# A decoder block's mixer: channel sums in pairs, two subtractions on GpSimd, the first convolution tap on ScalarE, and another order of VectorE's work

## Time and profile before

| | |
|---|---|
| median of 3 runs | 1147.88 us (1146.88 to 1148.16) |
| the profiled execution's own time | 1145.58 us |
| its span, first to last instruction | 1143.8 us |
| mean granted TensorE clock | 0.992 of full speed |
| TensorE matmul busy | 1102.6 us (96%) |
| VectorE busy | 334.3 us (29%) |
| ScalarE busy | 231.9 us (20%) |
| GpSimd busy | 23.0 us (2%) |
| HBM | 391 GB/s over the span |

### The profile page before, as it was taken

The page is one execution under the profiler, slowest core; times in us unless marked ns, Lnnn a source line. Parts: engine busy times, 40 slices in busy tenths (PEclk is TensorE's granted clock), DMA queues, the critical chain, the costliest instruction groups (busy, mean ns, idle before and its releaser), DMA issues.

```text
span 1143.8 us, 14032 instructions
## 1 busy us (share of the span) xinstructions
PE 1102.6 (96%) x5779; PEld 529.0 (46%) x5779; DVE 334.3 (29%) x639; ACT 231.9 (20%) x332; POOL 23.0 (2%) x34
## 2 busy tenths in 40 slices
PE   8999999999999999999999999999999999999997
PEld 8999998433333333333333333333333333333336
DVE  7899996311111111111111111111111111111127
ACT  7555454211110010110000010110100000000026
POOL 1300000000000000000000000000000000000011
PEclk9999999999999999999999999999999999999999
DMA  9984589899999999999999999999999999999991
GB/s 305 333 310 150 183 320 379 357 416 410 424 431 427 433 426 435 425 437 424 438 424 438 424 438 424 438 424 429 433 435 426 435 426 434 423 425 429 427 398 58
DMA packets 40959, 447.62 MB, mean 391 GB/s; under 512 B 3427, under 2 KB 3675, under 8 KB 21755
## 3 DMA queue, kind: packets, MB, share of 16 engines
q1 hardware_dynamic: 39924, 444.43, 93.5%
q0 software_dynamic: 672, 1.99, 0.7%
q10 hardware_dynamic: 327, 0.69, 0.2%
HBM read 446.05 MB, written 1.05 MB: 391 GB/s over the span
## 4 chain that ended last, share of the span: by engine, by line
PE 68%; DMA 28%; ACT 2%; DVE 1%; SPq 1%; issue 1%; DVEq 0%; ACTq 0%
PE ps L2038 23%; PE ps L2078 16%; DMA down_ring<-in_expert_w_down_dram 13%; DMA up_ring<-in_expert_w_up_dram 13%; PE ps L1765 6%; PE ps L2089 4%; PE ps L1775 3%; PE ps L1952 3%; DMA up_ring<-in_ple_gate_w_dram 2%; PE ps L1829 2%; PE ps L2194 2%; PE ps L1855 1%; ACT hT L985 1%; PE ps L1834 1%; PE ps L2066 1%; PE ps L2049 1%
## 5 line engine op out<-in xcount | busy, mean ns | idle before, releaser
L2038 PE MATMUL ps<-up_ring,hT 128*64 128x512 f32 x2032 | 447.2, 596 | 11.0 <-DMA up_ring<-in_expert_w_up_dram 10.6
L2038 PEld LDWEIGHTS ps<-up_ring,hT 128*64 128x64 f32 x2032 | 148.2, 138 | 301.5 <-issue 281.1
L2078 PE MATMUL ps<-down_ring,hT 128*64 128x512 f32 x992 | 229.8, 605 | 16.6 <-DMA down_ring<-in_expert_w_down_dram 10.1
L1515 DVE TENSOR_SCALAR extra<-ps 128x512 f32<-128x512 f32 x32 | 22.1, 692 | 698.0 <-PE ps L2049 698.0
L2078 PEld LDWEIGHTS ps<-down_ring,hT 128*64 128x64 f32 x992 | 68.1, 138 | 153.4 <-issue 139.6
L981 ACT ACTIVATE work<-ps 128x512 f32<-128x512 f32 x31 | 18.5, 596 | 424.1 <-PE ps L2049 424.1
L2089 PE MATMUL ps<-hT,extra 64*128 64x512 f32 x256 | 72.0, 640 | 0.8 <-DVE hT L1546 0.8
L1765 PE MATMUL ps<-h_hi,w_hi 128*128 128x256 f32 x288 | 70.2, 284 | 0.0
L1765 PE MATMUL ps<-h_lo,w_hi 128*128 128x256 f32 x288 | 69.9, 283 | 0.0
L791 ACT ACTIVATE w_hi<-up_ring 128x2048 fp32r<-128x2048 f32 x28 | 53.4, 1914 | 59.7 <-PE ps L1775 29.4
L481 DVE TENSOR_TENSOR w_lo<-up_ring,w_hi 128x2048 fp32r<-128x2048 f32 x28 | 64.3, 2301 | 3.8 <-ACT w_hi L791 3.6
(11 more groups left out here) (315 smaller groups left out, 804.6 us busy)
## 6 DMA issues: line engine op xcount, KB each, us to landing
up_ring<-in_expert_w_up_dram SPq DMA_DIRECT2D x47, 4096.0 KB, 27.0
down_ring<-in_expert_w_down_dram SPq DMA_DIRECT2D x63, 2048.0 KB, 18.3
up_ring<-in_expert_w_up_dram SPq DMA_DIRECT2D x31, 2048.0 KB, 15.1
up_ring<-in_w_in_dram SPq DMA_DIRECT2D x21, 1024.0 KB, 6.7
up_ring<-in_branch_w_dram SPq DMA_DIRECT2D x6, 1024.0 KB, 5.0
up_ring<-in_w_out_dram SPq DMA_DIRECT2D x4, 1024.0 KB, 6.8
up_ring<-in_expert_w_up_dram SPq DMA_DIRECT2D x4, 1024.0 KB, 24.2
up_ring<-in_ple_gate_w_dram SPq DMA_DIRECT2D x4, 1024.0 KB, 25.2
```

The lines of the kernel that those rows point to most:

```text
L1515: nc.vector.tensor_scalar(lin, ps[:, LIN, :], 1.0 + LIMIT, 1.0 - LIMIT, ALU.min, ALU.max).then_inc(lin_ready, 1)
L2038: ins = nc.tensor.matmul(ps[64 * g:64 * g + 64, GLU + side, :], xe[:, j, k % 4, k // 4, :], gated_columns(w, side, g), start=(k == 0), sto ...
L2078: last = nc.tensor.matmul(ps[64 * g:64 * g + 64, Y, :], actT[:, r, c, :], down_units[:, c, D * r + 512 * g:D * r + 512 * (g + 1)], start=( ...
```

## The change

- `mean_of_channels` takes two matmuls in place of four: GpSimd first adds tiles 0 and 1 to tiles 2 and 3 (`channel_pair_sums`, an addition of 128 x 512), once for `convT` and once for `squares`.
- The first mean is made behind branch unit 22 in place of ahead of it, the second behind unit 23 in place of behind 22. VectorE's `centred` stands behind its split of unit 24.
- Both `bias_rest` go from VectorE to GpSimd, the first ahead of the `rw` product; ScalarE's `round_biases(1)` goes from chunk a to behind chunk pool and its split of unit 8.
- The first tap of the convolution (scale and bias) is made by ScalarE; VectorE waits for it.
- ScalarE copies `pT` and `sguT` out of PSUM in place of VectorE.
- `v_norm` takes four `scalar_tensor_tensor` of 128 x 512 in place of six operations.
- `sgu_product` stands behind VectorE's split of unit 17, `yc_lo` behind that of unit 20, and `yc_hi` on ScalarE behind chunk 8.
- The semaphore `fold_ready` is replaced by a third count of `fills_ready`.

```diff
-BIAS_UNIT, SGU_UNIT = 16, 9
+SGU_PRODUCT_UNIT, YC_UNIT = 17, 20
...
+        channel_pairs = work[:, 2048:2560].rearrange("p (g t) -> p g t", g=2)
...
@@ gpsimd
+            def bias_rest(step):
+                rows = slice(0 if step == 0 else 2 * N_EXP, BIAS_PARTS * N_EXP)
+                pool.wait_ge(b_rounded, step + 1)
+                nc.gpsimd.tensor_tensor(b_rest[rows, :], b_rest[rows, :], b_parts[rows, :], ALU.subtract
+                                        ).then_inc(b_rest_ready, 1)
+            bias_rest(0)
             pool.wait_ge(mats_loaded, 64)
...
                                     ALU.mult).then_inc(rw_ready, 1)
+            pool.wait_ge(rw_ready, 1)
+            bias_rest(1)
+            def channel_pair_sums(src):
+                return nc.gpsimd.tensor_tensor(channel_pairs[:, :, :], src[:, 0:2, :], src[:, 2:4, :], ALU.add)
+            pool.wait_ge(b_rest_ready, 2)
+            pool.wait_ge(ycT_ready, 1)
+            pool.wait_ge(conv_step, CT * CONV_K)
+            channel_pair_sums(convT).then_inc(channel_pairs_ready, 1)
+            pool.wait_ge(mean_done, 1)
+            pool.wait_ge(sq_ready, 1)
+            channel_pair_sums(squares).then_inc(channel_pairs_ready, 1)
...
@@ scalar
                 if name == "a":
-                    round_biases(1)
+                    act.wait_ge(a_read, 1)
+                    act.wait_ge(taps_ready, 1)
+                    for c in range(CT):
+                        b = ROW["conv_b"] + c
+                        nc.scalar.activation(convT[:, c, :], y_pad[:, c, 0:T], ACT.Identity, bias=prm[:, b:b + 1],
+                                             scale=conv_taps[:, 0, c:c + 1]).then_inc(conv_step, 1)
                     continue
...
+                if n == 2:
+                    round_biases(1)
+                if n == 4:
+                    act.wait_ge(early_T_done, 1)
+                    nc.scalar.activation(pT[:, :, :].rearrange("p a t -> p (a t)"), ps[:, 4, :], ACT.Copy)
+                    nc.scalar.activation(sguT[:, :, :].rearrange("p h t -> p (h t)"), ps[:, 5, :], ACT.Copy
+                                         ).then_inc(sguT_ready, 1)
+                if n == 8:
+                    act.wait_ge(ycT_ready, 1)
+                    nc.scalar.activation(yc_hi[:, :, :], uT[:, :, :], ACT.Copy).then_inc(yc_hi_ready, 1)
...
             nc.scalar.activation(squares[:, :, :], convT[:, :, :], ACT.Square).then_inc(sq_ready, 1)
-            act.wait_ge(ycT_ready, 1)
-            nc.scalar.activation(yc_hi[:, :, :], uT[:, :, :], ACT.Copy).then_inc(yc_hi_ready, 1)
             split(BRANCH_UNIT0 + 3)
...
@@ vector
-                if u == 3:
-                    bias_rest(0)
...
-            for c in range(CT):
-                b = ROW["conv_b"] + c
-                nc.vector.tensor_scalar(convT[:, c, :], y_pad[:, c, 0:T], conv_taps[:, 0, c:c + 1],
-                                        prm[:, b:b + 1], ALU.mult, ALU.add).then_inc(conv_step, 1)
+            dve.wait_ge(conv_step, CT)
...
-                    own(nc.vector.tensor_scalar(v_sb[:, a, :], v_sb[:, a, :], vmv[:, 2 * a:2 * a + 1],
-                                                vrstd[:, a:a + 1], ALU.subtract, ALU.mult))
-                    own(nc.vector.tensor_tensor(v_sb[:, a, :], v_sb[:, a, :], v_gain, ALU.mult))
-                    last = nc.vector.tensor_tensor(v_sb[:, a, :], v_sb[:, a, :], v_shift, ALU.add)
+                    own(nc.vector.scalar_tensor_tensor(out=v_sb[:, a, :], in0=v_sb[:, a, :],
+                                                       scalar=vmv[:, 2 * a:2 * a + 1], in1=v_gain,
+                                                       op0=ALU.subtract, op1=ALU.mult))
+                    last = nc.vector.scalar_tensor_tensor(out=v_sb[:, a, :], in0=v_sb[:, a, :],
+                                                          scalar=vrstd[:, a:a + 1], in1=v_shift,
+                                                          op0=ALU.mult, op1=ALU.add)
...
-                if u == BIAS_UNIT:
-                    bias_rest(1)
...
-                if u == SGU_UNIT:
-                    dve.wait_ge(early_T_done, 1)
-                    nc.vector.tensor_copy(pT[:, :, :].rearrange("p a t -> p (a t)"), ps[:, 4, :])
-                    nc.vector.tensor_copy(sguT[:, :, :].rearrange("p h t -> p (h t)"), ps[:, 5, :]).then_inc(sguT_ready, 1)
+                if u == SGU_PRODUCT_UNIT:
+                    sgu_product()
+                if u == YC_UNIT:
+                    dve.wait_ge(yc_hi_ready, 1)
+                    nc.vector.tensor_tensor(yc_lo[:, :, :], uT[:, :, :], yc_hi[:, :, :].bitcast(F32),
+                                            ALU.subtract).then_inc(yc_lo_ready, 1)
...
             split(BRANCH_UNIT0)
-            dve.wait_ge(mean_done, 1)
-            nc.vector.tensor_tensor(convT[:, :, :], convT[:, :, :],
-                                    ps[:, 4:5, 0:T].to_broadcast([P, CT, T]), ALU.subtract).then_inc(centred, 1)
-            sgu_product()
             split(BRANCH_UNIT0 + 1)
-            dve.wait_ge(yc_hi_ready, 1)
-            nc.vector.tensor_tensor(yc_lo[:, :, :], uT[:, :, :], yc_hi[:, :, :].bitcast(F32),
-                                    ALU.subtract).then_inc(yc_lo_ready, 1)
...
             split(BRANCH_UNIT0 + 2)
+            dve.wait_ge(mean_done, 1)
+            nc.vector.tensor_tensor(convT[:, :, :], convT[:, :, :],
+                                    ps[:, 4:5, 0:T].to_broadcast([P, CT, T]), ALU.subtract).then_inc(centred, 1)
             dve.wait_ge(chunk_read, N_CHUNKS - 1)
             gate_branch(0)
...
@@ tensor
+            def mean_of_channels(bank):
+                for c in range(2):
+                    last = nc.tensor.matmul(ps[:, bank, 0:T], mean_mat[:, :], channel_pairs[:, c, :], start=(c == 0),
+                                            stop=(c == 1))
                 return last
...
-                    if u == BRANCH_UNIT0 - 1:
-                        pe.wait_ge(conv_step, 4 * CONV_K)
-                        pe.wait_ge(yaT_ready, 1)
-                        mean_of_channels(4, convT).then_inc(mean_done, 1)
...
                 if i == 0:
-                    pe.wait_ge(sq_ready, 1)
-                    mean_of_channels(5, squares).then_inc(var_done, 1)
+                    pe.wait_ge(yaT_ready, 1)
+                    pe.wait_ge(channel_pairs_ready, 1)
+                    mean_of_channels(4).then_inc(mean_done, 1)
+                if i == 1:
+                    pe.wait_ge(channel_pairs_ready, 2)
+                    mean_of_channels(5).then_inc(var_done, 1)
```

More of the change, by code:

```diff
@@ L382, in build @@
         mean_done = sem("mean_done")
+        channel_pairs_ready = sem("channel_pairs_ready")
         centred = sem("centred")
@@ L395, in build @@
         first_copied = sem("first_copied")
-        fold_ready = sem("fold_ready")
         logits_done = sem("logits_done")
@@ L1125, in _ @@
             nc.vector.tensor_reduce(fold[:, :], ident[:, :].rearrange("p (c e) -> p e c", c=4), axis=AX,
-                                    op=ALU.add).then_inc(fold_ready, 1)
+                                    op=ALU.add).then_inc(fills_ready, 1)
             for a in range(TT):
@@ L1926, in _ @@
             w_out_tile(m + 1, 1, [1]).then_inc(w_used, 2)
-            pe.wait_ge(fold_ready, 1)
+            pe.wait_ge(fills_ready, 3)
             pe.wait_ge(x_ready, 2)
```

## The result

The changed kernel takes 1154.59 us (median of 6 runs, 1152.19 to 1156.03) against 1146.85 us for the kernel before on the same chips: ratio 1.0063, 95% interval 1.0053 to 1.0072, so 7.2 us slower (6.1 to 8.3); the two medians differ by 7.7. The forecast was 4.2 us slower, 1152.1 us, its range 1148.5 to 1156.0 us.

The account below looks back on a forecast made before the run. TensorE was taken to bound the mixer, VectorE 3 to 5 us ahead, then the DMA stream. VectorE's lateness of 7.9 less 0.8 us, through layer norm's chain, gave +4.2 us: 1152.1 us, range 1148.5 to 1156.

Parts of the forecast that it names:

- Step 3: `bias_rest(0)` on GpSimd, 44.1 to 48.5 us, makes VectorE's taps stand: +4.4 us, and the `rw` product +0.5.
- Step 4: `bias_rest(1)` on GpSimd, 56.7 to 61.1 us, holds VectorE +4.4 us; TensorE stands 3.2 us for unit 8.
- the cushion: VectorE's 2.61 us of idle time ahead of 54.33 us in the kernel before, forecast to be used up.
- Step 5: VectorE's operations spared and put in front, together -0.8 us; the split of unit 22 starts at 147.1 us.
- Rival A: GpSimd is in nobody's way and VectorE keeps its lead: -1.6 us, 1146.3 us; chance 0.14.
- rival B: Only TENSOR_TENSOR stands, taps run beside GpSimd: +1.9 us, 1149.8 us; chance 0.15.
- rival C: Worse: a bf16 input costs GpSimd more, or TensorE's clock falls: up to +8 us, 1156 us; chance 0.13.
- Step 7: TensorE stands from 170.7 to 172.1 us ahead of unit 26, before at 167.90: +4.2 us, nothing changed behind it.
- Step 6: Layer norm's chain: first pair sum 1.15 us, done at 150.4; `centred` done at 156.0, `yb_lo` at 172.1 us.
- The sign that I had set for being wrong: GpSimd waits through a whole row of VectorE instructions, making `b_rest_ready` and ScalarE's split of unit 9 late; no size.
- Step 2: First tap on ScalarE: four activations of 1.58 us, done at 38.75 us, VectorE 1.6 us later.
- Step 1: Means: eight float32 matmuls become four, -1.73 us on TensorE.

Follow-up runs that it names:

- e1: The changed kernel with both `bias_rest` back on VectorE: 1149.04 us, ratio 1.0017 to the kernel before.
- e7: As e6, with `yb_lo` ahead of `gate_branch(2)` and of the split of unit 26 in VectorE's list: 1145.37 us, ratio 0.9989.
- e5: The changed kernel, with VectorE waiting for GpSimd's first pair sum ahead of the split of unit 22: 1152.39 us, ratio 1.0051.
- e10: The changed kernel with `bias_rest` on VectorE, and VectorE waiting for GpSimd's first pair sum ahead of unit 22's split: 1146.62 us, ratio 0.9992.
- e2: The changed kernel with means from four tiles in the new places and no pair sums on GpSimd: 1151.32 us, ratio 1.0034.
- e4: The kernel before with only both `bias_rest` on GpSimd and `round_biases(1)` behind chunk pool: 1148.56 us, ratio 1.0012.
- e3: The changed kernel with `bias_rest` back on VectorE and means from four tiles: 1146.52 us, ratio 0.9995.
- e11: As e3, with an idle GpSimd subtraction of two float32 tiles where `bias_rest(0)` was and a memset near the start: 1149.85 us, ratio 1.0025.
- e8: The changed kernel with the first tap back on VectorE: 1153.21 us, ratio 1.0055.
- e6: The changed kernel with `bias_rest` and both pair sums on VectorE: 1145.48 us, ratio 0.9985.

## Why the prediction came out as it did

**The place and the mechanism: right.** Step 3: VectorE held 4.4 us, measured 5.00 for a tap of 0.47, 4.5. Step 4: the cushion is used up, unit 8's split starts at 62.3 us by the sum, 62.99 measured; TensorE stands 3.2 by the sum, 3.0 measured. Step 5: unit 22's split at 147.1, measured 147.89. Rival A falls by the tap of 5.00 us and by e1, rival B by the same tap. Of rival C the clock came true, 0.72 after the first stand; the bf16 input didn't: 4.46 us. Step 7's one for one between the mixer's end and the kernel's is right: the last addition ahead of the experts starts between 202.61 us (e7) and 210.43 (the changed kernel), and from there to the end of the span it is 939.6 to 941.6 us in all thirteen profiles.

**Step 6 failed.** The first pair sum was to wait for one split and then hold VectorE 1.15 us, done at 150.4. It waited for three, and was done at 155.7. `centred` followed at 157.0 in place of 154.8, and TensorE stood 2.8 us ahead of the mean, which I had at nothing; the 1.4 us that step 7 has it stand ahead of unit 26 are hardly there in return (0.1 us in the window of 174 to 176 us). From the rows before I had read "GpSimd waits for the running instruction, then gets its turn"; two cases of it in the earlier trace rows, but neither beside a row of splits without a gap. Unit 26 started at 175.10 in place of 172.1. Of these 3.0 us, VectorE had 0.8 at unit 22 already, 1.4 came at `centred`, and 0.5 at the reciprocal, which waited for the root, behind TensorE's second mean; the rest are small steps. By the runs the stand is worth 1.4 us in the changed kernel (e5), and 2.8 in e1, clock included (e10).

The sign that I had set for being wrong, GpSimd kept waiting through a whole row of VectorE instructions, did come, and twice, but not at `bias_rest`, where I had put it. That the time lies in the range all the same is in part luck: the room above 1154 us was rival C's, whose main term, a bf16 input that costs more, didn't come, and it was filled by a stand that no rival had. The forecast itself is 2.5 us below the measured median, and short of the 7.2 us by 3.0.

**Step 2 was too small**: ScalarE's four taps took 2.09 us, not the 1.58 of L871. They read SBUF, and L871 reads PSUM; in the changed kernel's trace L927, from SBUF as well, takes 2.08 for four, and L889, from PSUM, 1.54 to 1.57. They also started at 37.80 us in place of 37.1, so VectorE's taps began 1.3 us later than in the sum, of which 0.8 is left at unit 22.

```profile
37.80 2.09 ACT xs L868 x4
```

**Step 1 was right and beside the point.** A mean of two matmuls takes 0.88 us undisturbed in place of 1.73, but the way the saving was bought, GpSimd beside a saturated VectorE, costs 3.3 us (e2 against the changed kernel) even net of it.

**What one profile is worth.** The forecast started from one profiled execution and from a median of three runs, 1147.88 us; the median of six is 1146.85. Against the kernel before, the start of unit 26 and the ratio of the runs agree for the changed kernel (7.2 and 7.2 us). Over all the runs the trace's difference is between 0.8 us too small (e5) and 1.8 too large (e10); e4 has 2.6 by the traces and 1.4 by the runs. So a start time "against the kernel before" is good to 1 or 2 us.

One thing that differs from execution to execution is the first rounding of the expert biases on ScalarE, which waits for a load. It starts at 22.79 us in the kernel before and between 23.62 and 26.36 in the twelve other profiles.

```profile
22.79 1.16 ACT L814 ACTIVATE b_rest<-b_rest,one 96x1024 f32<-96x1024 f32 x1 [1.23 <-DMA b_rest<-in_expert_b_up_dram]
```

In the changed kernel, where VectorE leads, the chain goes back to this load, and the product ahead of the first tap starts at 36.10 us in place of 34.16:

```profile
11.41 13.88 DMA b_rest<-in_expert_b_up_dram
```

In e3, where TensorE leads as in the kernel before, a rounding 2.3 us later costs nothing: TensorE's chain is later by 0.45 us from its first unit on (the kernel before, then e3), which is so ahead of any rounding, and unit 26 by 0.56.

```profile
12.12 4.27 PE ps L1733 x32
```

```profile
12.57 4.28 PE ps L1744 x32
```

**Open.** What decides whether GpSimd gets in between two VectorE instructions that follow one another. It got in between a split and a tap or two taps (at 41.3 us in the changed kernel, at 45 in e11), and not between two others: the `rw` product of the changed kernel stood from 51.04 through taps, a split and the first pool sum. The kind of its inputs is not it (e11). In nine of the thirteen profiles the `rw` product got in just ahead of the second pool sum (in the kernel before, ahead of the third), where VectorE's instructions don't overlap (the next starts 0.03 us after the last one's end, while splits of 2.29 us start 2.20 apart); but in e2, e5 and e11 it got in among the taps, which do overlap. And the first tap's share (e8), and when a stand of TensorE brings its clock down (e1 and e8 against the changed kernel).

## What to carry to other kernels

An engine with 2% busy is not a free engine: before work goes to GpSimd, look at what VectorE does at the same time, and if it is saturated with two-input instructions in SBUF, count GpSimd's time into VectorE's. If GpSimd's result is wanted soon, leave it a gap: one wait of the busy engine was worth 2.8 us in e10 and some 1.4 in e5. And when a small sum saves TensorE time, try the busy engine itself first: on VectorE it cost 0.7 us where GpSimd took 1.3 and the stands, and e6 and its variant e7 are the only kernels here that are faster than the one before.

## What the runs showed that I had not expected

GpSimd can be kept out for a whole row of instructions: 7.56, 7.56 and 7.55 us for a sum of 1.30, in three kernels, each time through exactly three splits. And a GpSimd instruction that only writes costs VectorE's two-input instructions nothing: 3.54 us of memset beside taps that keep their 0.477 us. It isn't harmless to all: a `tensor_scalar` of 0.75 us took 1.84 beside the memset of e11.
